# Gate weights' remainders by VectorE; the mixer's shift and scale sums by TensorE in four column groups; GpSimd keeps angles and filter taps

## The reference

```python
# first block
p = h @ w_in[l]
p_rwkv, q, k, v, gate_logits = jnp.split(p, IN_SPLITS, axis=-1)
y_a = rwkv7_bidirectional(p_rwkv, ...) @ w_o_rwkv[l]
y_b = neighbourhood_attention_2d(q, k, v, ...) @ w_o_na[l]
g_a, g_b = jnp.split(jax.nn.sigmoid(gate_logits + b_gate[l]), 2, axis=-1)
x = x + (g_a * y_a + g_b * y_b) @ w_out[l]
x = x + hierarchical_moe(rmsnorm(x, norm2_g[l]), ...)
# second block
silu_c, silu_cc = jax.nn.silu(c), jax.nn.silu(c_ctx)
sh1, sc1, g1, sh2, sc2, g2 = jnp.split((silu_c @ w_mod[l] + b_mod[l])[:, None, :], N_MOD, axis=-1)
csh1, csc1, cg1, csh2, csc2, cg2 = jnp.split(silu_cc @ w_mod[l] + b_mod[l], N_MOD, axis=-1)
h, hc = modulate(x, norm1_g[l], sh1, sc1), modulate(ctx, norm1_g[l], csh1, csc1)
```

## Time and profile before

| what | value |
| --- | --- |
| time, median of 3 runs | 1982.47 us (1979.17 to 1986.29) |
| the profiled execution's own time | 1987.91 us |
| its span in the trace | 1986.1 us |
| PE busy | 1814.6 us, 91% |
| DVE busy | 1015.8 us, 51% |
| ACT busy | 641.8 us, 32% |
| POOL busy | 430.0 us, 22% |
| core stage, merge stage | 235 to 580 us, 580 to 738.5 us |

### The profile page before, as it was taken

How to read it: one execution, slowest core, us unless ns; L and a number is a source line. 1 busy time by engine, 2 the same in 40 slices (tenths; PEclk the granted TensorE clock), 3 DMA queues, 4 the chain that set the end, 5 groups by cost and what they waited for, 6 DMA issues and landing times. The chain is left out here.

```text
span 1986.1 us, 44848 instructions
## 1 busy us (share of the span) xinstructions
PE 1814.6 (91%) x19103; PEld 1351.5 (68%) x19103; DVE 1015.8 (51%) x1815; ACT 641.8 (32%) x1217; POOL 430.0 (22%) x546
## 2 busy tenths in 40 slices
PE   7999999999979776998889999998999999999998
PEld 5776667777757553333347777677877787888886
DVE  7565444454457782111137765656667675323334
ACT  5555434434323221211134553012113253313321
POOL 1000245434449651111100000003232001101100
PEclk9999999899989877999989999999998999999999
DMA  6232111111146559999985210630001234332331
GB/s 217 79 99 69 59 55 35 35 30 40 40 175 248 169 171 356 410 409 410 406 332 187 61 58 26 212 112 15 23 14 67 108 107 128 98 100 89 96 106 43
DMA packets 77293, 272.64 MB, mean 137 GB/s; under 512 B 11574, under 2 KB 14006, under 8 KB 75440
## 3 DMA queue, kind: packets, MB, share of 16 engines
q1 hardware_dynamic: 64976, 238.64, 34.2%
q10 hardware_dynamic: 6336, 18.61, 2.8%
q0 software_dynamic: 5792, 12.64, 1.7%
HBM read 253.42 MB, written 24.12 MB: 140 GB/s over the span
## 5 line engine op out<-in xcount | busy, mean ns | idle before, releaser
L216 DVE TENSOR_TENSOR weights_lo<-ring,weights_hi 128x1024 fp32r<-128x1024 f32 (+1 forms) x125 | 152.5, 1221 | 151.7 <-ACT weights_hi L212 149.4
L212 ACT CAST weights_hi<-ring 128x1024 fp32r<-128x1024 f32 (+1 forms) x134 | 137.0, 1025 | 242.8 <-PE ps L242 232.3
L241 PE MATMUL ps<-wide_b_round,weights_hi 128*128 128x512 f32 (+1 forms) x368 | 136.9, 372 | 0.0
L240 PE MATMUL ps<-mlp_hi,weights_hi 128*128 128x512 f32 (+1 forms) x327 | 121.4, 371 | 1.1 <-DVE weights_lo L216 1.1
L242 PE MATMUL ps<-mlp_hi,weights_lo 128*128 128x512 f32 (+1 forms) x327 | 120.5, 368 | 0.0
L241 PE MATMUL ps<-mlp_lo,weights_hi 128*128 128x512 f32 (+1 forms) x327 | 120.4, 368 | 0.0
L4412 POOL TENSOR_TENSOR h_scaled<-h_scaled 128x512 f32<-128x512 f32 x32 | 33.8, 1055 | 299.4 <-ACT h_scaled L4386 299.4
L240 PE MATMUL ps<-h_tail,weights_hi 128*128 128x512 f32 x232 | 91.5, 394 | 0.7 <-DVE weights_lo L216 0.6
L240 PE MATMUL ps<-wide_a_round,weights_hi 128*128 128x512 f32 x216 | 91.7, 424 | 0.0
L242 PE MATMUL ps<-h_tail,weights_lo 128*128 128x512 f32 x232 | 91.0, 392 | 0.0
L241 PE MATMUL ps<-h_tail_rest_round,weights_hi 128*128 128x512 f32 x232 | 90.4, 390 | 0.0
(11 more groups left out here) (654 smaller groups left out, 4322.2 us busy)
## 6 DMA issues: line engine op xcount, KB each, us to landing
ring<-stream_in SPq DMA_DIRECT2D x207, 512.0 KB, 3.6
moe_ring<-stream_in SPq DMA_DIRECT2D x112, 512.0 KB
wide_b<-stream_in SPq DMA_DIRECT2D x32, 512.0 KB
w_mod<-w_mod_in ACTq DMA_DIRECT2D x24, 512.0 KB, 4.5
xT<-w_mod_in SPq DMA_DIRECT2D x16, 512.0 KB, 4.4
gates_parked<-gates_late SPq DMA_DIRECT2D x14, 256.0 KB, 2.1
na_rel<-rel_in POOLq DMA_DIRECT2D x4, 640.0 KB, 4.6
mod_acc<-mod_part ACTq DMA_DIRECT2D x5, 512.0 KB, 6.7
```

The source lines that it names most:

```text
L212: act.copy(self.hi[:, i % self.n, at:], w[:, at:]).then_inc(self.cast.sem, self.cast.up())
L216: ins = eng.tensor_tensor(self.lo[:, i % self.n, at:], self.unit(i)[0][:, at:], self.hi[:, i % self.n, at:], ALU.subtract)
L240: pe.matmul(out, left[0], right[0], start=start, stop=False, **kw)
L241: pe.matmul(out, left[0], right[1], start=False, stop=False, **kw)
```

## The change

1. Core stage: of the 16 gate rests POOL keeps units 0 to 3; the other 12 go to DVE (`rest_weights(t, place)`): "early" between `keep_state` and `keep_output`, "late" ahead of `keep_bonus`, and in round 1 ahead of the level-2 update. ACT's roundings and leavings stand at new places (GATE_ACT), mostly one earlier.
2. Merge stage: shift and scale sums for c and c_ctx are made by PE. silu(c) and silu(c_ctx) stand in columns 0 and 1 of a 32-column tile (the rest zero); for each of 16 chunks, four plain float32 matmuls (`mods`, 32x256 out, one per column group of 32) add into one PSUM bank. 12 chunks come after halves 4 to 15, two each after outs 0 and 1. Only the gate's 8 sums stay on DVE (L1984). `wm` has six buffers, `mod_acc` 0.77 MB instead of 2.5 MB, saved once.
3. POOL gives all weight rests, `mix` and `mix_rest` of the merge stage to DVE; it keeps the scaling of v, the angles and the taps.
4. The network's first layer comes after half 1 instead of ahead of half 0; the layers share the halves' three banks (HALVES, `spot`). SP issues the network's inputs first, the DFT table after the first 16 units; ACT rounds three units ahead of the w_mod issues.
5. At the end of the experts' stage PE picks shift and scale out of the kept sums with 16 matmuls of 2 columns; only the gate's row is still reduced by `mod_sums`.

```diff
-GATE_MID = {0: ((0,), (2,)), 1: ((2,), (4,)), 2: ((4,), (6,)), 3: ((), (7,)), 4: ((7,), (9,)), 5: ((), (10,)), 6: ((10,), (12,)),
+GATE_ACT = {(0, "turned"): (0, 2), (0, "end"): (1, 3), (1, "early"): (2, 4), (1, "middle"): (3, 5), (1, "end"): (4, 6), (2, "end"): (5, 7),
+GATE_REST = {(1, "early"): 4, (1, "late"): 5, (2, "early"): 6, (3, "early"): 7, (3, "late"): 8, (4, "early"): 9, (5, "early"): 10, (5, "late"): 11,
...
+                def rest_weights(t, place):
+                    if (t, place) in GATE_REST:
+                        u = GATE_REST[t, place]
+                        dve.wait_ge(w_rounded.sem, w_rounded.at(u + 1))
+                        dve.wait_ge(w_rested.sem, w_rested.at(u))
+                        dve.tensor_tensor(w_lo[:, slot(u), :], k.ring[:, slot(u), :], w_hi[:, u % 2, :], ALU.subtract).then_inc(
+                            w_rested.sem, w_rested.up())
...
+MOD_PE, MOD_Q, MOD_RING = 2, UNIT // 4, 6
+HALVES = [("half", 0), ("half", 1), ("layer", 0)] + [("half", n) for n in (2, 3, 4)] + [("layer", 1)] + [("half", n) for n in range(5, 16)]
+MOD_AFTER = {("half", n): 1 for n in range(4, 16)} | {("out", 0): 2, ("out", 1): 2}
+MOD_LAST = [0, 1, 2, 2, 2, 1, 0, 0]
...
-        def half_bank(n):
-            return n % 3
+        def spot(*event):
+            return HALVES.index(event) % 3
...
+                def mods(*event):
...
+                    for _ in range(MOD_AFTER.get(event, 0)):
+                        n, chunk = chunk, chunk + 1
+                        r, i = divmod(n, DB)
+                        if n == 0:
+                            pe.wait_ge(silu_done.sem, silu_done.at(2))
+                        pe.wait_ge(mod_in[n % MOD_RING].sem, mod_in[n % MOD_RING].at(16 * (n // MOD_RING + 1)))
+                        for q in range(4):
+                            mm = pe.matmul(k.ps[32 * q:32 * q + 32, 3, r * MOD_Q:(r + 1) * MOD_Q], silu[:, i, :], wm[:, n % MOD_RING, q * MOD_Q:(q + 1) * MOD_Q],
+                                           start=i == 0, stop=i == DB - 1, skip_group_check=True)
+                        mm.then_inc(mod_used.sem, mod_used.up())
...
                 w.rest(dve, 0)
+                w.rest(dve, 1)
                 first_sums()
                 group_norm(0)
                 weigh(0)
+                w.rest(dve, 2)
...
                     weigh(8 + i)
-                    mod_steps(8 + i)
+                    mix(i)
+                    if i:
+                        mix_rest(i - 1)
+                mix_rest(7)
+                w.rest(dve, 10)
                 dve.wait_ge(x_in.sem, x_in.at(16))
                 for i in range(8):
+                    if i and 10 + i < 16:
+                        w.rest(dve, 10 + i)
                     w.wait(dve, 8 + i)
                     dve.tensor_tensor(k.xT[:, i, :], k.xT[:, i, :], k.ps[:, i, :], ALU.add).then_inc(x_done.sem, x_done.up())
                     if i > 1:
                         norm.add(dve, i - 1)
-                    mod_steps(16 + i)
+                    for n in range(sum(MOD_LAST[:i]), sum(MOD_LAST[:i + 1])):
+                        mod_sum(n)
...
-                rest(1)
-                rest(2)
...
                 angles(0)
-                pool.wait_ge(a_done.sem, a_done.at(1))
-                rest(3)
                 angles(1)
                 pool.wait_ge(a_done.sem, a_done.at(2))
-                for i in range(8):
-                    mix(i)
-                    if i:
-                        mix_rest(i - 1)
-                rest(10)
-                mix_rest(7)
-                for i in range(8):
-                    if i and 10 + i < 16:
-                        rest(10 + i)
-                    if i % 2:
-                        fold(i // 2)
+                for t in range(NT):
+                    fold(t)
```

More of the change, by code:

```diff
@@ L1541, in _ @@
                                     norm_sums(1, 2, s)
+                        if t == 1 and lv == 2:
+                            rest_weights(t, "early")
                         if t == N and lv in (3, 4):
@@ L1718, in stage_merge @@
             tap_ready, tap_copied, tap_chain, both_done = (k.sig(x) for x in ("tap_ready", "tap_copied", "tap_chain", "both_done"))
[L1719 to L1724, removed]
+            mod_in, mod_used, mod_done, mod_kept, mod_saved = ([k.sig(f"mod_landed{i}") for i in range(MOD_RING)],
+                                                               *(k.sig("mod_" + x) for x in ("used", "summed", "kept", "saved")))
+            silu_done = k.sig("mod_silu")
+            chunks = DB * (MOD_PE + 1)
+            assert sum(MOD_AFTER.values()) == DB * MOD_PE and sum(MOD_LAST) == DB
             @block.tensor
@@ L1753, in tap, with half @@
                     mm.then_inc(tap_ready.sem, tap_ready.up())
-                def half(n, first):
+                def half(n):
                     i, e = divmod(n, 2)
@@ L1803, in _ @@
                         tap(i // 2)
+                    mods("out", i)
                 logits(7)
@@ L1830, in net_copy @@
                     act.wait_ge(a_ready.sem, a_ready.at(n + 1))
-                    act.activation(net[rows, 1, :], k.ps[rows, 3, :], ACT.Identity, bias=k.col("hy_b2" if n else "hy_b1", 0, 0, rows.stop)).then_inc(
+                    act.activation(net[rows, 1, :], k.ps[rows, spot("layer", n), :], ACT.Identity, bias=k.col("hy_b2" if n else "hy_b1", 0, 0, rows.stop)).then_inc(
                         a_copied.sem, a_copied.up())
@@ L1957, in weigh, with mix, mix_rest @@
                         dve.wait_ge(b_in.sem, b_in.at(16))
-                    dve.tensor_tensor(x, x, k.ps[:, half_bank(n), :], ALU.mult).then_inc(h_done.sem, h_done.up())
+                    dve.tensor_tensor(x, x, k.ps[:, spot("half", n), :], ALU.mult).then_inc(h_done.sem, h_done.up())
+                def mix(i):
+                    dve.wait_ge(h_done.sem, h_done.at(8 + i + 1))
+                    dve.tensor_tensor(gate(i), gate(i), gate(8 + i), ALU.add).then_inc(m_done.sem, m_done.up())
+                def mix_rest(i):
+                    dve.wait_ge(rounded.sem, rounded.at(i + 1))
+                    dve.tensor_tensor(mix_parts(i)[1], gate(i), mix_parts(i)[0], ALU.subtract).then_inc(rested.sem, rested.up())
                 def y_rest(b):
@@ L1971, in _ @@
                 weigh(2)
+                w.rest(dve, 3)
+                weigh(3)
                 group_norm(3)
-                weigh(3)
-                dve.wait_ge(k.used, k.after(3))
+                weigh(4)
                 w.rest(dve, 4)
-                weigh(4)
                 weigh(5)
```

201 lines of the change are left out of this document (102 added, 99 removed).

## The result

The changed kernel takes 1958.8 us (median of 4, 1951.29 to 1963.63), the kernel before 1980.88 beside it: a ratio of 0.9881, 95% interval [0.9841, 0.992]. Timed again later it gave 1962.05 us and 0.9885 [0.987, 0.9901], that is 0.0115 x 1984.63 = 22.8 us less, with 20 to 26 inside the interval. 1955 was forecast. All medians and ratios here leave out one execution, of `both_moved`, that took 2533 us at a mean clock of 0.647.

What follows compares the result with a forecast made beforehand. PE bounds the core stage nearly alone; in the merge stage it waits, mostly for DVE. Merge -28.5, core +1.9, experts -1 sum to -27.6: from 1982.47 to 1954.9, say 1955 us; 8-in-10 range 1944 to 1971.

Steps and rivals of the forecast that it cites:

- Start: Merge stage: half 0 starts at 583.7 us, when g_up's product ends, instead of 594.6; lead 10.9 us.
- Halves 2 to 5: Merge stage: PE waits 1.2 and 1.6 us for weigh and then the first angles; lead falls to 5.5 us.
- The PE sums: Merge stage: 0.6 us a chunk; 12 chunks before the outs cost 7.2 us, lead -1.5 us when halves end.
- rival (a): PE sums: column groups don't overlap at 256 columns; 1.71 us a chunk, 17.8 us more, 1973 us; chance 0.10.
- Out 0: Merge stage: weigh(15) is ready 0.8 us after the last half; out 0 takes 5.6 us, lead 10.5 us.
- Tail: Merge stage after out 7: 5.5 us remain of 17.8; lead 28.6 us.
- Core stage: Core stage: rests moved to DVE cost +1.9 us in sum, bounds -5 and +15.
- Rival (c): Core stage: DVE's rests are not covered, 12 us more than counted; 1967 us; chance 0.08.
- Experts' stage: Stage's end: 1.8 MB less come back and two reductions go; -1 us, bounds 0 and -4.
- Rival (b): Merge stage's halves: DVE becomes the bound, 4 us a half instead of 3.4; 1961 us; chance 0.10.
- (d): PE sums: chunks run one after another at the lower clock, 3.4 us each, 45 us more; 2000 us; chance 0.03.
- (e): Merge stage: nothing changes, PE's waits come back elsewhere through the ring's units or x's 2 MB; 1980 us; chance 0.03.

Runs made afterwards that it cites:

- both_moved: Changed kernel with ACT's first six w_mod chunks issued after the first net_copy, and DVE's late rests and round 1's early rest placed later; 1951.56 us, ratio 0.9817.
- run 9: The changed kernel timed once more, unchanged, against the kernel before; 1962.05 us, ratio 0.9885.
- Experiment 6: Changed kernel, but ACT issues the first six chunks of w_mod after the first net_copy instead of ahead of the square root; 1962.15 us, ratio 0.9865.
- experiment 3: Changed kernel with all four matmuls of 14 of the 16 chunks in the first column group; 1976.64 us, ratio 0.9956.
- core_before: Changed kernel with the core stage (tables, DVE's and POOL's rests) of the kernel before; 1957.0 us, ratio 0.9868.
- mods_one_group: Changed kernel with 14 of 16 chunks sending all four matmuls to one column group instead of one to each; 1976.64 us, ratio 0.9956.
- pool_keeps: Changed kernel, but in the merge stage POOL keeps weight rests 1 to 3 and 10 to 15, mix and mix_rest; sums stay on PE; 1959.42 us, ratio 0.9872.
- layer1_late: Changed kernel with later w_mod issues, DVE's rests moved later, and the network's second layer behind half 5 instead of half 4; 1948.31 us, ratio 0.9824.

## Why the prediction was right, and where it was not

The direction and most of the sum were right: -27.6 us forecast, -22.8 measured. By its steps, in us from the merge stage's start where nothing else is said:

- **Start.** First product 3.1 us after the stage's start, 3.7 forecast; no wait for hy_w (0.8 us in run 9), and layer 0 took 1 us.
- **Halves 2 to 5.** This step was mis-sized. The end of `weigh(0)` was put at 11.5 us and came at 15.0; PE waited 4.8 us instead of 1.2 (a wait for `weigh` beyond 2 us was among the signs that would make the forecast wrong), and 36 products took 11.2 us instead of 8.4 because the clock fell behind the wait. The norm's chain was in time: DVE was ready at 10.4. I had priced ACT's six w_mod issues as work ahead of the square root, but they were issued beside the roundings (at 572.2 to 575.3) and cost ACT 0.2 us at most, ahead of a wait of 3.1 us. What they cost was the gates' transfer, whose 12.2 us I had not looked at, and which the change itself issues 1.9 us later than before. Experiment 6 shows the chunks' part of it. The step's second part, that the angles would hold half 5, had the chain right and its end too early: the sine was there at 26.6, because POOL's eight angle instructions took 14.5 us, not 13.4, and ACT ended the sine 0.9 us after them, for which the forecast had left next to nothing. In the changed kernel this was only a tie, since PE came late; it became the wait when the first was removed. Half 5 began at 27.9, 26.0 forecast.
- **The PE sums.** 0.64 us for a chunk in its row, and rival (a) is gone: experiment 3 shows the overlap. But the forecast's 0.6 had to hold the changes of form as well. With its chunk a half takes 3.52 us (chunks begin at 615.48 and 619.00) where 3.4 was forecast; 12 halves with 0.12 more each make 1.4 us. The halves end at 68.6, 65.3 forecast.
- **Out 0.** It waited 0.26 us for a forecast 0.8 and ended 74.6 us after the stage's start, 71.7 forecast. The losses from the two steps above are still there.
- **Outs 1 to 7.** 51.2 us, PE never idle, at full clock; 52.7 forecast.
- **Tail.** 4.2 us for 5.5. With it the stage ends after 130.0 us, exactly the sum, which is luck: the errors are +2.9, -1.5 and -1.3.
- **Core stage.** +1.9 forecast; +3.4 and +3.6 by the ratios (uncertain by 5 and 4), +0.8 to 1.7 by PE's idle time. The late rests delay `keep_bonus` by about 1 us, as forecast, but in three waits instead of four: PE waits 1.8 us in two and 1.0 in one. Rival (c), 12 us more, is excluded.
- **Experts' stage.** -1 forecast, which did not come. From the merge stage's end to the span's end it is 1247.6 us before and 1247.3, 1248.9 and 1243.7 in the two executions of the changed kernel and `core_before`: no gain to be seen. The wait for the sums' return is gone, but PE waits 3.1 us there for the experts' rows (acc), as the step feared.
- **Rival (b)** did not come, since DVE was idle between halves (1.50 us before `weigh` 15). Rivals (d) and (e) are excluded by the waits and the ratio.

Merge -28.5, core +1 to +3.5, nothing behind: -25 to -27.5, with -22.8 measured and -20 to -26 inside its interval. The rest is not resolved. What stays open is why the clock of the core stage differs between executions of one program. It moves the total by more than the core part does: ten runs of `mods_one_group` go from 1960.5 us at a mean clock of 0.974 to 1982.7 at 0.964.

## What to carry to other kernels

If two engines are slow together, look first at the one whose instructions stretch the other's: with 32 sums less on DVE, POOL's `mix` took 1.29 us instead of 2.09, and moving POOL's own work as well was worth 2.3 us of the stage, which the total doesn't show. When a wait is removed, list every chain that ends at the same place with its own time (here the first `weigh` at 15.0 us, with PE at the second layer only at 26.9, and the sine at 26.6): the second was hidden behind the first by 0.2 us, and the stage became shorter only when the sine's user was moved too. When transfers are put in a new order, look at the time to landing of each one that is used soon, also when what changed stands in another queue. For a change below 1%, read the idle time of the bounding engine stage by stage; the length of a long stage goes with the clock.

## What was not expected of the hardware

- The same program's core stage took 337.2 us at a clock of 0.97 and 347.2 at 0.94.
- The contention between DVE and POOL works both ways: a DVE sum of 128x1024 takes 1.27 us with POOL idle and 2.86 in the mean in `pool_keeps`, POOL's 128x512 takes 1.29 and, beside DVE's, 2.27, and DVE's `weigh`, which reads PSUM, 0.69 in both kernels.
- A wait of 4.8 us of PE cost another 2.8 us in products at half clock; in `layer1_late`, with no wait above 1.1 us behind its first instruction, the stage had a clock of 1.00 from end to end.
